# A fourth place for split weights, and another order of work at both ends of the last attention

## The reference, cut to what matters

```
c_kv = rms_norm(h[..., :256]); k_rope = rope(h[..., 256:])
kv   = einsum('bsc,chd->bshd', c_kv, w_up)          # 16 heads x (128 key + 128 value)
c_q  = rms_norm(x @ w_dq, q_norm)                   # 384 columns
q    = einsum('bsc,chd->bshd', c_q, w_uq)           # 16 heads x (128 + 64)
s    = (q_nope . k_nope + rope(q_rope) . k_rope) * scale, causal, softmax
mix  = o.reshape(B, S, 2048) @ w_o
x    = layer_norm(alpha * x + mix)
x    = layer_norm(alpha * x + 0.5 * swiglu(x)); gate = sigmoid(x @ w_gate + b)
x    = layer_norm(alpha * x + gate * (p @ w_proj))
```

## Time and profile before

| | |
|---|---|
| time, median of 3 runs (lowest to highest) | 1580.15 us (1578.21 to 1580.59) |
| the profiled execution: its own time / its span | 1577.2 us / 1575.1 us |
| TensorE busy | 1522.5 us, 97% of the span |
| VectorE / ScalarE / GpSimd busy | 938.9 / 784.9 / 179.7 us |
| mean granted TensorE clock | 0.990 |

### The profile page before, as it was taken

One profiled execution on the slowest core, in us unless ns is written; L12 is line 12 of the kernel. 1 busy time (PEld: TensorE's weight loads), 2 busy tenths in 40 slices (PEclk: granted clock), 3 DMA queues, 4 the chain that ended last, 5 costly groups with the idle time before them and its releaser, 6 DMA issues.

```text
span 1575.1 us, 22060 instructions
## 1 busy us (share of the span) xinstructions
PE 1522.5 (97%) x8444; PEld 1320.6 (84%) x8444; DVE 938.9 (60%) x1214; ACT 784.9 (50%) x935; POOL 179.7 (11%) x52
## 2 busy tenths in 40 slices
PE   8999999999999999899899999899999999999997
PEld 6878888888888887798788888788888887888885
DVE  6564365666556667414566667866667444666667
ACT  4446445444444444655444445554446654544455
POOL 1014211000010001350100001200004441100001
PEclk9999999999999999999999999899999999999999
DMA  8544446655555554532465555465555334565552
GB/s 298 184 134 160 137 160 193 218 194 190 185 188 192 192 195 131 168 133 87 136 209 192 192 193 194 158 209 192 192 191 164 111 108 134 191 209 186 186 201 80
DMA packets 186861, 274.35 MB, mean 174 GB/s; under 512 B 9953, under 2 KB 137057, under 8 KB 186722
## 3 DMA queue, kind: packets, MB, share of 16 engines
q1 hardware_dynamic: 182848, 261.72, 50.2%
q10 hardware_dynamic: 3954, 11.80, 2.3%
HBM read 272.44 MB, written 1.05 MB: 174 GB/s over the span
## 4 chain that ended last, share of the span: by engine, by line
PE 84%; DVE 9%; ACT 4%; issue 1%; DMA 1%; POOL 0%; ACTq 0%; SPq 0%; DVEq 0%
PE bank L633 22%; PE bank L635 11%; PE bank L506 7%; PE bank L508 7%; PE bank L507 7%; PE acc L506 6%; PE acc L507 6%; PE acc L508 6%; DVE w_lo L1528 3%; ACT w_hi L1100 2%; PE acc L768 2%; PE acc L502 2%; PE bank L656 1%; PE bank L661 1%; PE bank L667 1%
## 5 line engine op out<-in xcount | busy, mean ns | idle before, releaser
L1528 DVE TENSOR_TENSOR w_lo<-w_raw,w_hi 128x2048 fp32r<-128x2048 f32 (+1 forms) x210 | 479.9, 2285 | 207.8 <-ACT w_hi L1178 121.6
L633 PE MATMUL bank<-xT,w_hi 128*128 128x512 f32 x1520 | 379.9, 392 | 0.0
L463 POOL TENSOR_TENSOR w_lo<-w_raw,w_hi 128x2048 fp32r<-128x2048 f32 (+2 forms) x42 | 175.5, 4182 | 1362.1 <-ACT w_hi L1100 1362.1
L633 PEld LDWEIGHTS bank<-xT,w_hi 128*128 128x128 f32 x1520 | 276.1, 189 | 51.3
L1178 ACT ACTIVATE w_hi<-w_raw 128x2048 fp32r<-128x2048 f32 x145 | 276.5, 1907 | 0.0
L1100 ACT ACTIVATE w_hi<-w_raw 128x2048 fp32r<-128x2048 f32 (+4 forms) x107 | 194.3, 1819 | 91.7 <-PE bank L508 61.3
L635 PEld LDWEIGHTS bank<-xT,w_lo 128*128 128x128 f32 x1520 | 207.4, 190 | 14.8
L635 PE MATMUL bank<-xT,w_lo 128*128 128x256 f32 x1520 | 211.9, 282 | 0.0
L506 PE MATMUL bank<-w_hi,xT 128*128 128x512 f32 x384 | 153.7, 400 | 4.4 <-DVE w_lo L1528 2.5
L506 PE MATMUL acc<-w_hi,hTh 128*128 128x512 f32 x400 | 156.2, 391 | 0.0
L507 PE MATMUL acc<-w_lo,hTh 128*128 128x512 f32 x400 | 156.2, 391 | 0.0
(11 more groups left out here) (214 smaller groups left out, 2091.0 us busy)
## 6 DMA issues: line engine op xcount, KB each, us to landing
w_raw<-in_ffn_w_in SPq DMA_DIRECT2D x176, 512.0 KB, 4.4
w_raw<-in_ffn_w_out SPq DMA_DIRECT2D x88, 512.0 KB, 4.2
w_raw<-in_w_in SPq DMA_DIRECT2D x52, 512.0 KB, 4.7
w_raw<-in_fox_w_in SPq DMA_DIRECT2D x24, 512.0 KB, 4.5
w_raw<-in_w_ffn_gate SPq DMA_DIRECT2D x22, 512.0 KB, 4.5
w_raw<-in_w_ffn_up SPq DMA_DIRECT2D x22, 512.0 KB, 4.6
w_raw<-in_w_ffn_down SPq DMA_DIRECT2D x22, 512.0 KB, 4.2
w_raw<-in_ple_w_gate SPq DMA_DIRECT2D x16, 512.0 KB, 4.2
```

The source lines that it names most:

```text
L463: pool.tensor_tensor(w_lo[slot][:, 0:cols], w_raw[slot][:, 0:cols], w_hi[slot][:, 0:cols].bitcast(F32), ALU.subtract).then_inc(w_lo_done[s ...
L633: pe.matmul(out, wh[:, k, m], both, start=k == 0, stop=False)
L1528: nc.vector.tensor_tensor(w_lo[slot][:, 0:cols], w_raw[slot][:, 0:cols], w_hi[slot][:, 0:cols].bitcast(F32), ALU.subtract)\
```

## The change

There are four places for the split weights (`HRING = 4`) and still three for the raw ones. Outside the SwiGLU loops a unit takes the place that was last used longest ago, so its high split waits for unit u - 4 and not u - 3; inside the loops the units keep to three places as before. The space for it comes from three buffers: `kz` (zero-padded keys) moves into the shared arena, as `mkz` with four tiles for the sparse attention and as `fkz` with eight for fox, whose zeros GpSimd now writes during SwiGLU layer 1; `krT` gets a place of its own there; `pin` shares the space of `rope_ret`, so that the first load of p is issued by ScalarE just ahead of SwiGLU layer 0 and not at the start. At the head of each SwiGLU layer ScalarE splits unit 3 ahead of the tanh and not behind it.

In the last attention unit kv_up 3 is loaded ahead of uq 0, and `kv(3)` runs right behind the transposes of c_q, ahead of the wait for their evacuation and of `uq(0)`. Behind the heads the order is: `turn_o(7)`, the first unit of output chunk 0 and that of chunk 1 for both tiles, the transposes of p (into bank 6), then the second units of both chunks for tile 0 and then for tile 1. ScalarE evacuates p's transposes (`keep_p`) between the high splits of the third and the fourth output unit. VectorE adds both chunks tile by tile (`by_tile`).

```diff
--- before.py
+++ after.py
+HRING = 4
...
     chunks("dq", w["mla_w_dq"], KD, 0, 1, n=QL)
     kv_up(2)
-    uq(0)
     kv_up(3)
-    for g in range(1, 8):
+    for g in range(8):
         uq(g)
...
-    for c in range(2):
-        for k0 in (8, 12):
+    for k0 in (8, 12):
+        for c in range(2):
             dense(f"mla_ob{c}", w["mla_w_o"], k0, 4, c * CH, CH)
...
+    slots, before = [], []
+    for u, unit in enumerate(units):
+        last = [max((v for v in range(u) if slots[v] == s), default=-1) for s in range(HRING)]
+        late = unit[3] is None and u - unit_at[unit[0]][0] >= 5
+        slots.append(slots[u - 3] if late else min(range(HRING), key=lambda s: last[s]))
+        before.append(last[slots[u]])
...
-        w_hi = [sb(f"w_hi{s}", UNIT, F32R) for s in range(RING)]
-        w_lo = [sb(f"w_lo{s}", UNIT, F32R) for s in range(RING)]
+        w_hi = [sb(f"w_hi{s}", UNIT, F32R) for s in range(HRING)]
+        w_lo = [sb(f"w_lo{s}", UNIT, F32R) for s in range(HRING)]
...
-        pin = sb("pin", T * PLE)[:, :].rearrange("p (t n) -> p t n", t=T)
+        pin = rope_ret
...
-        krT = kz[:, 0, 0]
+        krT = cm(S)
...
+                if u == unit_at["ffn1"][0] + 2:
+                    need("pool", "ffn_out", 0, 1)
+                    pool.wait_ge(w_lo_done[(u - 1) % RING], (u - 1) // RING + 1)
+                    pool.wait_ge(zeros_set, 3)
+                    pool.memset(fkz[64:P, 0], 0.0).then_inc(zeros_set, 1)
+                    pool.wait_ge(zeros_set, 4)
+                    pool.memset(fkz[0:64, 1], 0.0).then_inc(zeros_set, 1)
...
+        P_BANK = [3, 6]
...
+            def turn_p(l):
+                pe.wait_ge(p_loaded, 16 * (l + 1))
+                transposes(P_BANK[l], ("pT", l), ("pTf", l),
+                           [(j * S + t * P, pin[:, t, j * P:(j + 1) * P]) for t in range(T) for j in range(2)])
...
+                    kv(3)
                     for t in range(T):
                         need("pe", "cqT", t)
...
                     uq(0)
-                    kv(3)
                     uq(1)
...
-                    ob = tile_steps("mla_ob0", (4, 5), slot0=8)
+                    ob0, ob1 = (Chunk(f"mla_ob{c}", b, slot0=8) for c, b in ((0, (4, 5)), (1, (2, 3))))
+                    turn_o(7)
                     need("pe", "oT", 4)
                     need("pe", "oT", 5)
-                    ob[0]()
-                    turn_o(7)
+                    ob0.run(0)
+                    ob1.run(0)
+                    turn_p(1)
                     need("pe", "oT", 6)
                     need("pe", "oT", 7)
-                    ob[1]()
-                    ob[2]()
-                    chunk("mla_ob1", (2, 3), slot0=8)
-                pe.wait_ge(p_loaded, 16 * (l + 1))
-                transposes(3, ("pT", l), ("pTf", l),
-                           [(j * S + t * P, pin[:, t, j * P:(j + 1) * P]) for t in range(T) for j in range(2)])
+                    for t in range(T):
+                        ob0.run(1, tiles=(t,))
+                        ob1.run(1, tiles=(t,))
+                if l == 0:
+                    turn_p(0)
...
-                    if u >= RING:
-                        act.wait_ge(w_used, u - RING + 1)
-                    nc.scalar.activation(w_hi[u % RING][:, 0:cols], w_raw[u % RING][:, 0:cols], ACT.Copy)\
+                    if before[u] >= 0:
+                        act.wait_ge(w_used, before[u] + 1)
+                    nc.scalar.activation(w_hi[slots[u]][:, 0:cols], w_raw[u % RING][:, 0:cols], ACT.Copy)\
                         .then_inc(w_hi_done, 1)
...
-                split_to(u0 + 3)
+                split_to(u0 + 4)
                 first_tanh(u0 + 1)
-                split_to(u0 + 4)
...
-            load_p(0)
...
             load_norm(2)
+            load_p(0)
             ffn(0)
...
+                    keep_kv(3)
                     ahead("uq", 0)
                     keep_q(0)
-                    keep_kv(3)
...
                     keep_oT(7)
-                    ahead("mla_ob0")
+                    split_to(unit_at["mla_ob1"][1])
+                    keep_p(1)
+                    split_to(unit_at["mla_ob1"][1] + 1)
                 split_to(unit_at[f"ffn{2 + 2 * l}"][0] + 1)
                 root_table()
                 norm_and_turn(3 + 4 * l, early=unit_at[f"ffn{2 + 2 * l}"][0] + 2, b0=4)
...
+            def by_tile(stage, alpha, banks=(0, 1)):
+                split_to(unit_at[f"{stage}1"][-1] + 2)
+                def finish(t):
+                    add_chunk(stage, 0, t, banks, alpha)
+                    add_chunk(stage, 1, t, (2, 3), alpha)
+                return finish
...
                     rest_oT(7)
-                    ahead("mla_ob0")
-                    finish = update("mla_ob", 1.0, (4, 5))
+                    split_to(unit_at["mla_ob1"][1])
+                    rest_p(1)
+                    finish = by_tile("mla_ob", 1.0, (4, 5))
```

More of the change, by code:

```diff
@@ L298, in build @@
         fo = cf.tiles(T, D)
+        fkz = cf(2 * 8 * S).rearrange("p (a k n) -> p a k n", a=2, k=8)
         fsel_raw = fo.rearrange("p t (h n) -> p (t h) n", n=P)
@@ L623, in ffn, with wide @@
                 assert 3 * FI == len(unit_at[f"ffn{f}"])
-                def wide(slot, split, b):
-                    pe.wait_ge(w_lo_done[slot], split)
-                    wh, wl = (w[slot][:, :].rearrange("p (k m n) -> p k m n", k=KD, m=2) for w in (w_hi, w_lo))
+                def wide(u, split, b):
+                    pe.wait_ge(w_lo_done[u % RING], split)
+                    wh, wl = (w[slots[u]][:, :].rearrange("p (k m n) -> p k m n", k=KD, m=2) for w in (w_hi, w_lo))
                     for m in range(2):
@@ L636, in wide, with last_up @@
                     mm.then_inc(w_used, 1)
-                def last_up(slot, split):
-                    pe.wait_ge(w_lo_done[slot], split)
-                    wh, wl = (w[slot][:, :].rearrange("p (k m n) -> p k m n", k=KD, m=2) for w in (w_hi, w_lo))
+                def last_up(u, split):
+                    pe.wait_ge(w_lo_done[u % RING], split)
+                    wh, wl = (w[slots[u]][:, :].rearrange("p (k m n) -> p k m n", k=KD, m=2) for w in (w_hi, w_lo))
                     for m in range(2):
@@ L683, in turn_first, with down @@
                                [(m * S + t * P, hid[:, t, m * P:(m + 1) * P]) for m in range(2) for t in range(T)])
-                def down(slot, split, hh, hl, first, last, tiles=range(T)):
+                def down(u, split, hh, hl, first, last, tiles=range(T)):
                     if tiles[0] == 0:
-                        pe.wait_ge(w_lo_done[slot], split)
-                    wh, wl = (w[slot][:, :].rearrange("p (k n) -> p k n", k=2) for w in (w_hi, w_lo))
+                        pe.wait_ge(w_lo_done[u % RING], split)
+                    wh, wl = (w[slots[u]][:, :].rearrange("p (k n) -> p k n", k=2) for w in (w_hi, w_lo))
                     for t in tiles:
@@ L724, in step @@
                         pe.wait_ge(g_summed, i + sums0)
-                    wide((u0 + 2) % RING, i + ((u0 - 1) // RING + 1), 0)
+                    wide(u0 + 5, i + ((u0 - 1) // RING + 1), 0)
                     if first:
@@ L1362, in _, with keep_p @@
                            accum_out=stats[:, t:t + 1])
+                def keep_p(l):
+                    need("act", "pTf", l)
+                    go(("pTh", l), cTh[:, 0:2, :], bank[P_BANK[l]].rearrange("p (k n) -> p k n", k=2))
                 def keep_ckv():
@@ L1409, in keep_turned @@
                         if stage[4] == "k":
-                            keep_keys(("fT", stage), slice(j, j + 2), slice(0, S), src)
+                            keep_keys(("fT", stage), fkz, slice(j, j + 2), slice(0, S), src)
                         else:
@@ L1471, in _ @@
                 load_norm(4 + 4 * l)
-                need("act", "pTf", l)
-                go(("pTh", l), cTh[:, 0:2, :], bank[3].rearrange("p (k n) -> p k n", k=2))
+                if l == 0:
+                    keep_p(0)
                 ffn(2 + 2 * l)
@@ L1916, in update, with rest_p @@
                 return lambda t: add_chunk(stage, 1, t, (2, 3), alpha)
+            def by_tile(stage, alpha, banks=(0, 1)):
[4 more added lines that the diff above has]
+                return finish
+            def rest_p(l):
+                need("dve", "pTh", l)
+                did(nc.vector.tensor_tensor(cTl[:, 0:2, :], bank[P_BANK[l]].rearrange("p (k n) -> p k n", k=2),
+                                            cTh[:, 0:2, :].bitcast(F32), ALU.subtract), "pT", l)
             def add_chunk(stage, n, t, banks, alpha):
```

82 lines of the change are left out of this document (40 added, 42 removed).

## The result

The changed kernel takes 1582.05 us in the median of 20 runs (1576.69 to 1583.55), the kernel before 1578.8 (1577.42 to 1581.0): a ratio of 1.0016, 95% interval 1.001 to 1.0023. It is a little slower, by 0.16%, where I had forecast no measurable change with a lean of 0.6 us to the faster side. A second series gave 1.001 (1.0001 to 1.0019, 12 runs). The profiled execution took 1582.46 us and its span is 1580.5, 5.4 above the span before; the medians differ by 3.3, since the profiled execution of before was a quick one.

The account below looks back on a forecast made before the run. TensorE is busy 1522.5 of 1575.1 us, so only its waits and lowered clock can be won. Terms -4.1 - 0.5 - 0.9 + 1.6 + 3.7 - 0.4 = -0.6 took the median 1580.15 to 1579.5 us, range 1575.0 to 1584.8.

Parts of the forecast that it names:

- Step 1: First block: the fourth place lets high splits run earlier, shrinking TensorE waits and removing lowered clock behind one: -4.1 us.
- Step 2: Sparse attention's transposes: two waits for VectorE's product, 0.6 us in all, mostly go as its splits stand earlier: -0.5 us.
- Step 3: Embedding gate 0: a split that waited 1.34 us for TensorE starts earlier, shortening the chain to the layer norm: -0.9 us.
- Step 4: SwiGLU heads: third split ahead of the tanh delays TensorE, 0.75 each in layers 2 and 0, 0.1 in layer 4: +1.6 us.
- Step 5: Query head: three back-to-back GpSimd splits hold VectorE's small chain; +2.0 us of waiting and +1.7 of lowered clock: +3.7 us.
- Step 6: Behind the last heads: new order removes 2.6 us of waits, keep_p delays the fourth output unit's split by 2.2: -0.4 us.
- rival B: Slower, 1584.5 us, chance 0.15: clock low longer behind query head's 3.9 wait (+3.3), and low behind last heads' 2.2 wait (+1.7).
- A: Query head, faster: chain slips between GpSimd's splits without lowered clock, 4.2 us less, 1575.3; chance 0.25.
- C: First block, slower: high splits wait for loads (sign: they name DMAs), so the start gains nothing, 1583.6 us; chance 0.08.

Follow-up runs that it names:

- experiment 1: Changed kernel with the tanh put back ahead of the third split at each SwiGLU head: 1576.59 us, ratio 0.9982 to the kernel before.
- experiment 5: Changed kernel with 26 unread identity transposes added ahead of TensorE's wait for the normalised c_q: 1579.15 us, ratio 1.0004 to the kernel before.
- experiment 3: Changed kernel with evacuation of p's transposes moved behind the fourth output unit's split: 1577.82 us, ratio 0.9993 to the kernel before.
- experiment 6: Changed kernel with uq 0's low split given to VectorE: 1576.25 us, ratio 0.9987 to the kernel before.
- experiment 7: Changed kernel with old tanh order, old query order and later keep_p(1) together: 1570.84 us, ratio 0.9953 to the kernel before.
- 8: Kernel before with only the fourth place added, buffers moved for it, all orders as before: 1574.33 us, ratio 0.9974 to the kernel before.
- experiment 4: Changed kernel with three places (HRING = 3), all orders as changed: 1596.28 us, ratio 1.0107 to the kernel before.
- experiment 2: Changed kernel with the old query order (uq 0 ahead of kv_up 3, uq(0) ahead of kv(3)): 1578.68 us, ratio 1.0001 to the kernel before.
- 11: Changed kernel with experiments 1, 3 and 6, plus 48 unread transposes in the fox set-up's wait: 1568.73 us, ratio 0.993 to the kernel before.

## Why the prediction was wrong

The forecast of -0.6 us was +2.5 to +3.3 by the times and +5.4 between the two profiles. Step by step, against the profiles:

**Step 1 (-4.1) was too large, by 2.5 in the profile.** The waits came as worked out: the 0.8 is gone, and the 2.5 shrank to 1.04, where I had 0.9. GpSimd's split fell on the inverse square root, as I had put it (VectorE's L1862 took 4.58 us for 128x32), and not on the product as in the earlier trace rows. Two things were missed. The first is a new wait of 0.71 at 126. VectorE makes two low splits in a row there, before as after, only 2.3 us earlier now; TensorE, whose clock is no longer lowered ahead of it, gets there some 4 us earlier and has to wait for the first of them. The splits, first before, then after, and the new wait:

```profile
125.97 4.49 DVE L1528 TENSOR_TENSOR w_lo<-w_raw,w_hi 128x2048 fp32r<-128x2048 f32 x2
...
123.65 4.49 DVE L1556 TENSOR_TENSOR w_lo<-w_raw,w_hi 128x2048 fp32r<-128x2048 f32 x2
...
126.08 0.47 PE L524 MATMUL bank<-w_hi,xT 128*128 128x512 f32 x1 [0.71 <-DVE w_lo L1556]
```

All eleven profiles with four places, which have full clock over 117 to 122, have this wait (0.66 to 0.71), and the two with three places, whose clock is lowered there, do not: of the 1.7 won from the clock, 0.7 is given back at once. The second is that the 1.7 of lowered clock came back at 174. That one is the profiled execution's, and so are 0.3 us by which its first projection started later. From the first matmul of the first projection to layer 0 the ten other profiles with four places all take 236.3 us, this one 238.0, and the two with three places 239.9. By them the fourth place is worth 3.6 us up to layer 0 (steps 1 and 2 together: -4.6); that layer 0 starts anywhere from 246.1 to 247.3 in the ten is due to the start of the first projection, at 9.8 to 11.0.

**Step 2 (-0.5) was nearly nothing:** 0.51 of the 0.61 is left (L1934).

**Step 3 (-0.9) holds:** the stretch from the end of layer 2 to layer 3 is 1.0 shorter, 963.11 to 1011.93 against 962.28 to 1012.12, and TensorE's longest wait in it fell from 3.4 to 2.4. From layer 2's first wide matmul to layer 3 three other profiles with four places are 0.8 to 0.9 shorter than before, and the seven others, which lose 3.4 us and not 5.0 to the lowered clock over 985 to 1006, are 1.6 shorter. That clock, which I left alone, differs between executions too.

**Step 4 (+1.6) was the first mis-sized term: it is 2.5.** The mechanism is right and experiment 1 undoes it. I had set the delay at 0.75 in layers 0 and 2 and found 1.0: the wait that the profile prints is 0.85 to 0.93, and the first matmul behind it is late by the drain of the pipelined one ahead too (13.45 - 12.45). In layer 4 I had let the departed transposes of p pay for it, 0.1, and it costs 0.55.

**Step 5 (+3.7) was right in size and place: 3.7 to 3.9.** Of it 1.6 is longer waiting (3.64 against 2.05), and some 2.2 the lowered clock, on kv(3) for 1.8 and on the transposes of c_q ahead of it for the rest (8.7 us together, 6.5 in experiment 5); I had 2.0 and 1.7. The chain went on at 1222.7 (forecast 1222.9), the transposes at 1225.34 (1225.6), the wait was 3.64 (3.9). What I had wrong is which instructions are held: I thought of those with two SBUF inputs. Held were two TENSOR_SCALAR instructions with one input, L2048 and L1575, and the two-input ones came when GpSimd was done. The Trainium skill (GPSIMD Engine Reference, Key points) names instructions in a two-port mode beside those with two SBUF inputs. The trace fits that half of the rule as far as it goes: the two held have one input each, while their mode is not shown in it. Its numbers show that a small instruction is held until the whole split has ended.

**Step 6 (-0.4) is where the sign was lost: +0.7 up to layer 4 and +0.4 in it.** The new wait is 2.07 (forecast 2.2) and by the mechanism given; experiment 3 removes it. But I priced the clock behind it at nothing and kept 1.7 for rival B; without that the step would have read -1.0. It fell behind this wait in six of the seven profiles with it in them (not in that of experiment 6), the same 1.6 to 1.7 each. And GpSimd's split for layer 4 did hold the layer norm of tile 1 (L1636), for 0.4 (the 12.86 of experiment 1 against 12.45), which I had set off against p's transposes. The gain of the step, -2.6, was right: with the wait mended, layers 3 to 4 are 3.2 shorter by the new order (experiments 7 and 8), less the 0.4.

So no rival came true whole. Of B its second half did (the clock behind the 2.07 wait), not its first: behind the 3.6 wait 2.2 us were lost and not 5. A failed: the chain did not slip between the splits. C failed, though the sign that I gave for it is there: in the first 40 us five high splits wait for their loads, 7.6 us in all, where one did before, for 1.5. They did not undo the gain: the first block is 3.6 us shorter with them, and the fourth place alone makes the kernel 0.26% faster. ScalarE's waits for loads of `w_in` after:

```profile
ACT w_hi L1125 <- DMA w_raw<-in_w_in: 7.6, 5, 2.3
```

The sum over the steps as measured is -1.6 (1 and 2) - 1.0 + 2.5 + 3.7 + 1.1 = +4.7; the remaining 0.7 of the profiled 5.4 I did not trace to a wait. Of the 5.4, 2.0 (the stretch at 174 and the later start) belong to this execution. The change's gains (fourth place, last heads) are 0.47% by experiment 7; three details of order, each of which put a waiting or slow instruction ahead of one that TensorE wanted, took them back and 0.16% more. Whether experiment 1 really gained more than the 2.5 us of its waits stays open.

## What to carry to other kernels

When an in-order engine gets a new instruction with a wait (`keep_p`), list what is queued behind it and when that could have run: here a split that was ready 10 us earlier stood behind it. Keep a long GpSimd elementwise instruction off the time in which VectorE runs a chain that TensorE waits for, however small the chain's instructions are; one split moved to VectorE was worth 4.6 us. Price a new wait of TensorE of 2 us or more with the clock behind it, 1.7 to 2.2 us here, and judge a part of a change by undoing it alone: this change was a gain of 0.47% and a loss of 0.63% in one.

## What the runs showed of the hardware

- The lowered clock is not a fixed companion of a place. With the same waits, one execution has its stretch of some 3.4 us (1.7 lost) at 174, the next none there and one between 620 and 640. Behind the 3.6 us wait it fell in all four profiles that have it, and behind 4.3 in experiment 4; behind the 2.5 near 117 in both that have it; behind the wait of 2.07 near the end in six of seven; behind 2.05 to 2.17 at the query head in two of four (not before and in experiment 2, but in 7 and 8); behind the 2.3 ahead of layer 2 in two of thirteen; at the 1.6 near 755 in ten of thirteen (not in experiments 5, 6 and 11); behind the 1.3 near 625 in two of thirteen, and behind the 1.3 at 173 in one. So the length of the wait does not decide it alone. Two profiles can differ by 1.7 us for no reason of the kernel's, and a single pair of them is not enough to size a term of that order.
- Idle time of TensorE could be filled with transposes that nobody reads, 0.115 us each (3.00 us for 26), and the stretch behind ran at full clock: 5.9 us instead of 7.6 for 36 matmuls, and 1.00 instead of 0.66 over 650 to 660.
- A VectorE TENSOR_SCALAR on 128x2 values takes 0.17 us, and 3.25 when it is issued beside a GpSimd subtraction: it ends 0.03 us behind it. When another subtraction follows at once, the next instruction of the chain is held until that one has ended (2.58 us): here one VectorE instruction got through between two subtractions.
